# Layer 0 of a three-layer transformer kernel reordered, with its first feed-forward product split into reduced-precision passes, and attention steps of the last layer interleaved

## Time and profile before

| | |
|---|---|
| span of the profiled execution | 1378.0 us |
| its own time | 1379.8 us |
| TensorE (PE) | 1242.6 us, 90% |
| its weight loads | 1139.7 us, 83% |
| VectorE (DVE) | 795.6 us, 58% |
| ScalarE (ACT) | 502.3 us, 36% |
| GpSimd (POOL) | 370.9 us, 27% |
| moved by DMA | 258.14 MB, mean 187 GB/s |
| mean granted TensorE clock | 0.958 |

### The profile page before, as it was taken

How to read it: one execution, slowest core, us unless ns; L and a number is a source line. 1 busy time by engine, 2 the same in 40 slices (tenths; PEclk the granted TensorE clock), 3 DMA queues, 4 the chain that set the end, 5 groups by cost and what they waited for, 6 DMA issues and landing times.

```text
span 1378.0 us, 23730 instructions
## 1 busy us (share of the span) xinstructions
PE 1242.6 (90%) x10368; PEld 1139.7 (83%) x10368; DVE 795.6 (58%) x913; ACT 502.3 (36%) x654; POOL 370.9 (27%) x581
## 2 busy tenths in 40 slices
PE   1699998889989986889899999997989998899999
PEld 1587587778879966879799999796769998799998
DVE  4896886334463437964586533647765465555353
ACT  2221122111113433433555432446457743444341
POOL 7999653555414806920000000000000021000000
PEclk9899999999999998989999999998989999999999
DMA  8964666988774474406355445343332453355451
GB/s 322 362 216 155 227 213 225 333 285 301 284 289 161 154 259 160 155 21 244 122 172 182 184 183 181 131 146 109 123 122 92 154 184 123 123 184 184 157 210 62
DMA packets 118791, 258.14 MB, mean 187 GB/s; under 512 B 5056, under 2 KB 18656, under 8 KB 118560
## 3 DMA queue, kind: packets, MB, share of 16 engines
q1 hardware_dynamic: 86160, 185.78, 38.3%
q10 hardware_dynamic: 27584, 51.01, 10.1%
q0 software_dynamic: 4944, 19.83, 4.0%
HBM read 241.93 MB, written 14.68 MB: 186 GB/s over the span
## 4 chain that ended last, share of the span: by engine, by line
PE 67%; DVE 13%; DMA 9%; ACT 4%; issue 3%; POOL 3%; DVEq 0%; POOLq 0%; ACTq 0%
PE bank L1737 67%; DMA ada_slot<-in_ada_w 6%; DVE ada_acc L1233 4%; DVE big L1330 3%; POOL big L747 2%; DVE rstd L1243 1%; DMA memory_kv<-s_tables 1%; POOL big L740 1%; DVE ring_split L1281 1%; ACT ada_slot_split L831 1%; DMA ring<-in_w_ffn_down 1%; DVE h_in L1264 1%; DMA ring<-in_w_glu_a 1%; DMA ring<-in_w_ffn_up 1%; DVE ada_acc L1230 0%
## 5 line engine op out<-in xcount | busy, mean ns | idle before, releaser
L1737 PE MATMUL bank<-squares_split,ring_split 128*128 128x256 f32 x800 | 227.2, 284 | 0.0
L1737 PE MATMUL bank<-h_in,ring 128*128 128x256 f32 x832 | 197.6, 399 | 7.3 <-ACT h_in L792 7.2
L1737 PEld LDWEIGHTS bank<-h_in,ring 128*128 128x128 f32 x832 | 165.4, 201 | 32.8 <-issue 7.5
L753 POOL TENSOR_TENSOR y_cat<-y_cat,tmp 128x512 f32<-128x512 f32 x8 | 10.7, 1343 | 537.5 <-DVE tmp L1669 537.5
L1737 PEld LDWEIGHTS bank<-squares_split,ring_split 128*128 128x128 f32 x800 | 154.3, 193 | 0.0
L1233 DVE SCALAR_TENSOR_TENSOR ada_acc<-ada_slot,cact,ada_acc 128x512 f32<-128x512 f32 x168 | 133.9, 797 | 6.0
L1737 PE MATMUL bank<-ada_slot_split,ring_split 128*128 128x256 f32 x432 | 122.3, 283 | 0.0
L1737 PE MATMUL bank<-h_in_split,ada_slot_split 128*128 128x256 f32 x384 | 111.7, 291 | 8.0 <-DVE y_cat_split L1673 3.8
L1281 DVE TENSOR_TENSOR ring_split<-ring,ada_slot_split 128x2048 fp32r<-128x2048 f32 (+1 forms) x32 | 72.2, 2257 | 80.0 <-ACT ada_slot_split L831 80.0
L1737 PE MATMUL bank<-big_split,ring_split 128*128 128x256 f32 x352 | 100.3, 285 | 0.0
L831 ACT ACTIVATE ada_slot_split<-ring 128x2048 fp32r<-128x2048 f32 (+1 forms) x32 | 60.2, 1885 | 70.6 <-PE bank L1737 42.6
(11 more groups left out here) (409 smaller groups left out, 3565.2 us busy)
## 6 DMA issues: line engine op xcount, KB each, us to landing
ring<-in_w_fc SPq DMA_DIRECT2D x32, 2048.0 KB, 8.5
ada_slot<-in_ada_w ACTq DMA_DIRECT2D x22, 2048.0 KB, 12.6
ring<-in_w_in SPq DMA_DIRECT2D x19, 2048.0 KB, 7.9
ring<-in_w_ffn_gate SPq DMA_DIRECT2D x5, 2048.0 KB, 7.7
ring<-in_w_ffn_up SPq DMA_DIRECT2D x5, 2048.0 KB, 8.1
ring<-in_w_ffn_down SPq DMA_DIRECT2D x5, 2048.0 KB, 8.0
ring<-in_w_out SPq DMA_DIRECT2D x4, 2048.0 KB, 9.4
ring<-in_w_branch SPq DMA_DIRECT2D x3, 2048.0 KB, 7.7
```

Source lines behind the costliest of these rows:

```text
L753: pool.tensor_tensor(merged, merged, tmp3[:, 2 * p:2 * p + 2, :], ALU.add).then_inc(s("mga"), 1)
L1737: return pe.matmul(*args, skip_group_check=True, **kw)
```

## The change

The projections themselves and the last norm are left as they were. These things change:

- **Early chunks.** SP issues, before anything else, the small inputs, `x` and chunks 0 to 3 of `ada_w`, each with a place of its own (chunk 2 in `big`, chunk 3 in `ring2`); then the panels `av` and `ag` without a wait, the constants (from POOL before), and `q` behind job `ada3`. Chunks 4 to 23 are issued by ACT. For chunks 0 to 3 DVE adds six slabs and PE takes the other two straight from the weights (8 more matmuls of one column). The reciprocal of the first norm is done between chunks.
- **Taps.** DVE runs the taps of both pairs one behind the other and adds PE's part afterwards (`add_taps`). Chunks 5, 6 and 7 move behind the taps on DVE, and jobs `ada5`, `ada6` behind the scores on PE.
- **First feed-forward split.** `f1.0` becomes a split product with 16 new weight units, and norm 1 splits its output. The chunks of `ada_w` are spread: 10 to 15 by halves in `f1.0`, 16 to 21 in `f2.0`, 22 and 23 in `f1.1` of layer 1. S5 blocks 5 to 7 move one or two steps earlier in `f2.0`.
- **Attention.** `fk0` moves ahead of `kot`; `nr0`, `nr1` and `fk1` ahead of `cs0`. `nr4` and `nr5` move from behind `bg0` to behind `bg1` and `bg2`, on PE, ACT and DVE alike.
- **Merge.** The low parts of the merged branches 0 and 1 are made between the last two gate products.

Lines are cut to the changed ones; leading blanks are reduced in each hunk. Left out besides: the bookkeeping of semaphore counts, and the lines that move `ada5`, `ada6`, `root("nr4")` and the head means as told above.

```diff
@@ -40,7 +40,8 @@
-SW_ADA = 2
+EARLY_ADA = 4
+DVE_SLABS = 6
@@ -56,27 +57,33 @@
-ADA_AFTER = {1: 10, 2: 11, 3: 12, 5: 13, 6: 14, 7: 15, 9: 16, 10: 17, 11: 18, 13: 19, 14: 20, 15: 21}
+ADA_AFTER = {3: 10, 6: 11, 8: 12, 11: 13, 13: 14, 15: 15}
+ADA_LOAD_AFTER = {2: 12, 5: 13, 7: 14, 10: 15, 12: 16, 14: 17}
+ADA_HALVES = {0: (10, 0), 1: (10, 1), 2: (11, 0), 4: (11, 1), 5: (12, 0), 6: (12, 1), 7: (13, 0), 9: (13, 1),
+              10: (14, 0), 11: (14, 1), 12: (15, 0), 13: (15, 1)}
+S5_AFTER = {1: 1, 5: 2, 9: 3, 13: 4}
+SIDE_ADA = {0: 16, 1: 17, 3: 18, 4: 19, 5: 20, 6: 21}
+SIDE_S5 = {0: 5, 2: 6, 4: 7}
...
-    jobs = ["ada0", "ada1", "ada2", "ms0", "ada3", "av0", "ag0", "av1", "ag1", "ada4", "q0", "q1", "cv0", "ada5", "k0", "k1", "ada6",
-            "rot0", "rot1", "rot2", "rot3", "cv1", "va0", "va1", "sc0", "sc1", "sc2", "sc3", "g0",
+    jobs = ["ms0", "ada0", "ada1", "ada2", "ada3", "av0", "ag0", "av1", "ag1", "ada4", "q0", "q1", "cv0", "k0", "k1",
+            "rot0", "rot1", "rot2", "rot3", "cv1", "va0", "va1", "sc0", "sc1", "sc2", "sc3", "ada5", "g0", "ada6",
...
-            "wo0.0", "wt0.0", "kl0", "wt0.1", "ada7", "wo0.1", "ada8", "wo0.2", "ada9", "wo0.3", "ms1"]
+            "wo0.0", "ada7", "wo0.1", "wt0.0", "kl0", "wt0.1", "ada8", "wo0.2", "ada9", "wo0.3", "ms1"]
...
-        if j % 4 == 0:
-            k = j // 4 + 1
+        if j in S5_AFTER:
+            k = S5_AFTER[j]
...
-        if b < 2:
-            jobs.append(f"ada{22 + b}")
-        if b % 3 == 0:
-            k = 5 + b // 3
+        if b in SIDE_ADA:
+            jobs.append(f"ada{SIDE_ADA[b]}")
+        if b in SIDE_S5:
+            k = SIDE_S5[b]
@@ -89,10 +96,14 @@
-jobs += ["f1.1.0", "mkr0", "f1.1.1", "mkr1"] + [f"f1.1.{j}" for j in range(2, 16)]
+jobs += ["f1.1.0", "mkr0", "f1.1.1", "mkr1"]
+for j in range(2, 16):
+    jobs.append(f"f1.1.{j}")
+    if j in (5, 9):
+        jobs.append(f"ada{22 + j // 9}")
...
-jobs += ["gq0", "gk0", "ff", "gv0", "gv1", "la", "gg0", "gg1", "fq0", "fq1", "kot", "cs0", "cs1",
-         "nr0", "nr1", "at0", "at1", "fk0", "fk1", "go0", "gor0", "nr2", "nr3", "go1", "gor1",
+jobs += ["gq0", "gk0", "ff", "gv0", "gv1", "la", "gg0", "gg1", "fq0", "fq1", "fk0", "kot",
+         "nr0", "nr1", "fk1", "cs0", "cs1", "at0", "at1", "go0", "gor0", "nr2", "nr3", "go1", "gor1",
@@ -373,8 +384,15 @@
+def buffers_at(places):
+    return [split[name][:, o:o + 2048] for name, o in places]
...
+T_, B_, Y_ = buffers_at((("tmp", 0), ("big", 6144), ("y_cat", 0)))
+for i in range(16):
+    units.append((f"f1.0.{i // 2}", 256 * (i % 2), 256, ((T_, B_, Y_) * 4 + (T_, Y_) * 2)[i]))
+base = FC = len(units)
@@ -428,7 +446,7 @@
-SPLIT_NORMS = (3, 5, 6)
+SPLIT_NORMS = (1, 3, 5, 6)
@@ -527,17 +545,42 @@
+def ada_in(k):
...
+    return s(f"ada_in{k % 4}"), 16 * (k // 4 + 1)
...
+def ada_slot(k):
...
+    place = big[:, 4096:8192] if k == 2 else ring[2][:, :] if k == 3 else adas[k % 2 if k < 22 else 1][:, :]
+    return place.rearrange("p (k c) -> p k c", k=KT)
...
+def ada_source(k):
...
+    l, c = divmod(k, ADA)
+    return a["ada_w"][l][:, 512 * c:512 * c + 512].rearrange("(k p) c -> p k c", p=P)
...
+def ada_load(eng, k):
...
+    if k < EARLY_ADA + 2:
+        job_wait(eng, f"ada{k - EARLY_ADA}")
+    else:
+        eng.wait_ge(s("ada_acc"), k - 1 if k < 23 else k)
+    eng.dma_start(ada_slot(k), ada_source(k)).then_inc(ada_in(k)[0], 16)
...
+    sp.dma_start(prep[:, 0:192], a["s5_scal"]).then_inc(s("s5_in"), 16)
...
+    for k in range(EARLY_ADA):
+        sp.dma_start(ada_slot(k), ada_source(k)).then_inc(ada_in(k)[0], 16)
...
-            sp.wait_ge(s("ada_acc"), 2 * ADA)
+            sp.wait_ge(s("ada_acc"), 22)
@@ -570,9 +613,15 @@
-else:
-    sp.wait_ge(s("ada_acc"), (1, 3, 4)[i])
+elif name == "q":
+    job_wait(sp, "ada3")
...
+if name == "ag":
+    sp.dma_start(ident[:, :], a["ident"]).then_inc(s("const_in"), 16)
+    sp.dma_start(early[:, 1536:2176], a["rope"]).then_inc(s("const_in"), 16)
+    sp.dma_start(scanmask[:, :], a["scanmask"]).then_inc(s("const_in"), 16)
+    sp.dma_start(dreg[:, :], a["decay"]).then_inc(s("const_in"), 16)
+    sp.dma_start(s5c[:, :], a["s5_select"]).then_inc(s("const_in"), 16)
@@ -636,10 +668,6 @@
-pool.dma_start(early[:, 1536:2176], a["rope"]).then_inc(s("const_in"), 16)
-pool.dma_start(scanmask[:, :], a["scanmask"]).then_inc(s("const_in"), 16)
-pool.dma_start(dreg[:, :], a["decay"]).then_inc(s("const_in"), 16)
-pool.dma_start(s5c[:, :], a["s5_select"]).then_inc(s("const_in"), 16)
@@ -806,8 +834,16 @@
+    job_wait(act, "ro1")
+elif u == 1:
+    act.wait_ge(s("ry"), 2)
+elif u == 2:
+    job_wait(act, "wo0.3")
+elif u < FC:
+    job_wait(act, f"f1.0.{u - 3 if u < 13 else u - 2}")
+elif u == FC:
...
-elif u in (1, 2):
+elif u in (FC + 1, FC + 2):
@@ -836,11 +872,11 @@
-squares(0, False)
-for k in range(2, 6):
-    ada_load(act, k)
-root("ms0")
+squares(0)
+act.wait_ge(s("panel0"), 16)
+ada_load(act, 4)
...
+ada_load(act, 5)
@@ -903,9 +939,12 @@
+split_high(0)
+split_high(1)
...
+split_high(2)
@@ -918,24 +957,25 @@
-    if j in ADA_AFTER:
-        ada_load(act, ADA_AFTER[j] + 2)
-    if j % 4 == 0:
-        s5_weights_out(j // 4 + 1)
+    if j + 3 < FC:
+        split_high(j + 3)
+    if j in ADA_LOAD_AFTER:
+        ada_load(act, ADA_LOAD_AFTER[j])
+    if j in S5_AFTER:
+        s5_weights_out(S5_AFTER[j])
...
-        split_high(u)
-        if u == 2:
-            s5_weights_out(5)
+        split_high(FC + u)
+        if u in (2, 5, 9):
+            s5_weights_out(5 + u // 4)
...
-    if b == FC2 + 2:
-        s5_weights_out(6)
-s5_weights_out(7)
+    if b < 6:
+        ada_load(act, 16 + b)
@@ -983,6 +1023,7 @@
+ada_load(act, 22)
@@ -1011,6 +1052,10 @@
+if j == 3:
+    ada_load(act, 23)
+if j == 8:
+    act.wait_ge(s("ada_acc"), 24)
@@ -1217,21 +1261,25 @@
-def ada_acc(k):
-    dve.wait_ge(*ada_in(k))
-    if k >= 2:
-        job_wait(dve, f"ada{k - 2}")
-    w = adas[k % 2][:, :].rearrange("p (k c) -> p k c", k=KT)
+def ada_acc(k, first=0, end=KT):
...
+    n = DVE_SLABS if k < EARLY_ADA else KT
+    links = (DVE_SLABS - 1) * min(k, EARLY_ADA) + (KT - 1) * max(k - EARLY_ADA, 0)
+    if first == 0:
+        dve.wait_ge(*ada_in(k))
+        if k >= 2:
+            job_wait(dve, f"ada{k - 2}")
+    w = ada_slot(k)
...
-    for i in range(KT):
+    for i in range(first, min(end, n)):
...
-            dve.wait_ge(s("ada_part"), 7 * k + i)
+            dve.wait_ge(s("ada_part"), links + i)
...
-                .then_inc(s("ada_part") if i < KT - 1 else s("ada_acc"), 1)
+                .then_inc(s("ada_part") if i < n - 1 else s("ada_acc"), 1)
@@ -1304,8 +1353,10 @@
+    if k == 1:
+        rms("ms0")
...
-norm(0)
+norm(0, False)
@@ -1319,27 +1370,26 @@
-            if tap == 0 and j == 0:
+            if tap == 0:
...
-                if tap == 0:
-                    dve.wait_ge(s("cvadd"), 2 + i % 2)
-                else:
-                    dve.wait_ge(s("conv"), 2 * DVE_TAPS * j + 2 * tap + i % 2 - 1)
+                dve.wait_ge(s("conv"), 2 * DVE_TAPS * j + 2 * tap + i % 2 - 1)
...
+def add_taps(j):
...
+    dve.wait_ge(s("conv"), 2 * DVE_TAPS * (j + 1))
+    job_wait(dve, f"cv{j}")
+    tt(conv[:, 2 * j:2 * j + 2, :], conv[:, 2 * j:2 * j + 2, :], ps2(f"cv{j}"), ALU.add).then_inc(s("cvadd"), 1)
...
-ada_acc(5)
-dve.wait_ge(s("conv"), 2 * DVE_TAPS)
-job_wait(dve, "cv0")
-tt(conv[:, 0:2, :], conv[:, 0:2, :], ps2("cv0"), ALU.add).then_inc(s("cvadd"), 1)
-ada_mod(5)
-ada_acc(6)
+convolve(1, 0, DVE_TAPS)
+add_taps(0)
@@ -1351,15 +1401,15 @@
-ada_mod(6)
-job_wait(dve, "cv1")
-for i in range(2):
-    ts(conv[:, 2 + i, :], ps2("cv1")[:, i, :], col("conv_b", 2 + i), None, ALU.add).then_inc(s("cvadd"), 1)
-convolve(1, 0, DVE_TAPS // 2)
+add_taps(1)
+ada_acc(5)
+ada_acc(6)
...
-convolve(1, DVE_TAPS // 2, DVE_TAPS)
+ada_mod(5)
+ada_acc(7)
+ada_mod(6)
@@ -1385,36 +1435,50 @@
-for k in range(7, 10):
-    ada_acc(k)
-    if k > 7:
-        ada_mod(k - 1)
+ada_mod(7)
+ada_acc(8)
+ada_acc(9)
+ada_mod(8)
...
+split_low(0)
...
+split_low(1)
+split_low(2)
...
-for k in range(10, 23):
-    ada_acc(k)
-    if k > 10:
-        ada_mod(k - 1)
+for j in range(16):
+    if j + 3 < FC:
+        split_low(j + 3)
+    if j in ADA_AFTER and j < 15:
+        ada_mod(ADA_AFTER[j])
+    if j in ADA_HALVES:
+        k, half = ADA_HALVES[j]
+        ada_acc(k, 4 * half, 4 * half + 4)
+ada_acc(16)
+ada_mod(15)
...
-    split_low(2 * (b - FC2))
-    split_low(2 * (b - FC2) + 1)
+    if b >= 4:
+        ada_mod(13 + b)
+    split_low(FC + 2 * (b - FC2))
+    if b == 3:
+        ada_acc(18)
+    split_low(FC + 2 * (b - FC2) + 1)
...
-    if b == FC2:
-        ada_mod(22)
-        ada_acc(23)
-    if b == FC2 + 1:
-        ada_mod(23)
+    if b == 2:
+        ada_acc(17)
+        ada_mod(16)
+    elif 4 <= b < 7:
+        ada_acc(15 + b)
+ada_mod(21)
@@ -1496,6 +1560,14 @@
+if j in (1, 2):
+    ada_acc(22, 4 * j - 4, 4 * j)
+elif j in (5, 6):
+    ada_acc(23, 4 * j - 20, 4 * j - 16)
+    if j == 6:
+        ada_mod(22)
+elif j == 10:
```

(70 more changed lines are left out.)

54 lines of the change are left out of this document (16 added, 38 removed).

## The result

The changed kernel takes 1358.86 us, the median of 4 runs (1357.81 to 1359.69), against 1378.41 for the kernel before on the same chip: a ratio of 0.9858, 95% interval 0.9827 to 0.9889. That is 20 us less where I had forecast 54 less, and outside my range (1306 to 1349).

| stage | before | after | change | forecast |
|---|---|---|---|---|
| up to the output projection's main run | 186.37 | 183.31 | -3.1 | -11 |
| from there to the end of `f1.0.0` | 51.0 | 55.0 | +4.0 | -0.5 |
| rest of `f1.0` | 151.6 | 122.2 | -29.4 | -44 |
| `f2.0` | 110.45 | 119.65 | +9.2 | +1 |
| from there to the first S5 product | 23.15 | 19.75 | -3.4 | -3 |

A forecast was written before the change was run, and what follows sets the result against it. PE was taken as held up by layer 0's modulation chunks, the start's chunk chain and the taps, and as the bound in split matmuls. Terms -11 - 3 + 2.5 - 49 + 5 + 1 - 3 + 2.5 + 1 = -54 gave 1326 us, range 1306 to 1349.

The forecast's parts named there:

- POOL needs 20 us a block and gets 27: First feed-forward: GpSimd's preparation of each S5 block was put at 20 us, with 27 us available, so not late.
- Chunk 4 ... lands near 45: Start to the taps: chunk 4, loaded once `av` is in (33), lands near 45; first tap point taken as 61.5.
- The extra 4.5 us of two weight units' splitting ... stand beside PE's last job: nothing: Output projection: splitting two more weight units on DVE and ACT, 4.5 us, runs beside PE's last job and costs nothing.
- Output projection, -3: Output projection: chunk 9 loads earlier against its use, so its wait and the slow matmuls behind go: -3 (0 to -4).
- the S5 table: After the second feed-forward: ACT's awaited table comes before the norm is through; -3 of a 4.7 us gap (0 to -4).
- 5 for late landings: First feed-forward: +5 us (0 to +20) added because 338 GB/s would be needed, against 388 at best and 297 before.
- two signs of being wrong: PE waiting for low parts or ACT for panels in `f1.0`, over 10 us in sum; or the `rot3` gap over 15.
- (a): Rival: the feed-forward becomes transfer-bound at 297 GB/s: 1335 us, or 1342 with the same in `f2.0`; chance 0.12.
- (b): Rival: DVE isn't held up in layers 0 and 2; early 15.5 us kept, head loop gives 8.5: 1313 us; chance 0.10.
- (c): Rival: the split doesn't pay; the rest of the chain keeps `f1.0` at 7.0 us a job: +19, 1345 us; chance 0.08.
- (d): Rival: slower; units of `f1.0` aren't prepared ahead and their steps run in series: about 1405 us; chance 0.04.
- (e): Rival: early chunks land no sooner on one queue, so the start stays at 55: +7, 1333 us; chance 0.06.

## Why the prediction was wrong

It was wrong by 34 us in four places, in order of size.

- **"POOL needs 20 us a block and gets 27."** The step that failed, and the largest. It is a duration read under a VectorE with 74.6 us of work in 160 and carried to one with 85 in 131, most of it long instructions. It needed 27.6 to 33.8 in `f1.0`. I added up each engine's busy time and found room on all of them, and asked nothing about two engines at once, though the 30.2 us of block 7 stood in the trace before. Cost: 13.0 us in `f1.0` and 8.9 in `f2.0`, by the kernel with GpSimd's work shortened.
- **"Chunk 4 ... lands near 45."** It landed at 54.1, and the main run came 7.9 us later than forecast. I gave it 12 us from an issue at 33, though chunks at the start had taken 16.5; issued at 35.8 beside `ag` and the constants, it took 18.3. With the wait for it filled the main run comes at 173.6, where I had 175.
- **"The extra 4.5 us of two weight units' splitting ... stand beside PE's last job: nothing."** One low part stood ahead of the residual on VectorE, and `wo0.3` waits for that: some 3.5 us by the estimate above. I had priced the instruction and not what is queued behind it.
- **Output projection, -3** for chunk 9. Its sum is no longer late, as forecast, but the bias behind it still waits for job `ada9`, and the residual behind the bias. With bias and low part both behind the residual, the stage is 6 us shorter; of that the bias has some 2.5.

Right within 1 us were `f2.0` without GpSimd (110.7 against 111.5) and the S5 table (-3.4 against -3). That `f1.0` with GpSimd out of the way took 117.9, forecast 118.9, is in part luck. Its sum held 2.5 for norm 1, where `f1.0.0` took 8.75 us against 8.83 before, and 5 for late landings, which weren't what came (304 GB/s were carried in 112.4 us without the low parts). In their place stood the wait of 1.8 us for a chunk's sum and a clock of 0.66 to 0.70 around it. The sum of all that follows was right within 1 too (+2.6 against +3.5), where the 13 us gap ahead of `go0` was 10.4. The clock was not: 0.92 in `f1.0`, with the gaps, against 0.98. Of my two signs of being wrong, the gap at `rot3` (15.2, over 15) came; the other named low parts and panels in `f1.0`, and so missed GpSimd. Of the rivals none was the case: (a) falls with 304 GB/s carried, (b) with the attention undone and with 3.1 us kept of the early 15.5, (c) had the rest of the chain as pace-setter but not GpSimd, and (d) and (e) did not come.

Left open is why the S5 scan took up to 4 us longer in some kernels: the granted clock was low in the two longest (0.90 and 0.92 at 87.2 and 87.0 us), but it was 0.91 in the kernel before, which took 83.3.

## What to carry to other kernels

A duration read in one stage holds only under the neighbours that it had there: before moving long two-operand work to VectorE, look whether GpSimd has a chain of its own in that stretch, and price that chain by its slowest case; here the trace before had one, 30.2 us beside seven of 19.2 to 22.7. Such a hold-up leaves no idle gap, only longer instructions; compare the mean of one form between stretches. And when extra work is put on an in-order engine, ask first what stands behind it, then how long it is; the cheapest filling here was to move work into a wait already there (10 us of scalars into 9.4 us, for one moved line).

## What the runs showed of the hardware

A GpSimd instruction of 128x256 took 0.62 us alone, up to 2.89 under a VectorE subtraction of 128x2048 (2.3 to 2.75), 1.60 under a copy of the same size (1.23) and 0.95 to 1.21 under subtractions of 128x512. The same copy takes half the subtraction's time. And the 12 one-column matmuls of chunk 3, written in the trace as 24, took 5.3 us (35.76 to 41.04) at a granted clock of 0.50, the lower level (1.2 GHz), with TensorE in nothing but short work and gaps ahead of them: the dearer of the two prices that I had (5.6 and 2.9).
